# Layer 1 of a diffusion trunk: the prompt's attention, the new keys and the gate rows between the value projection's matmuls

## The reference, cut to what matters

```
q, k, v = split(h @ w_qkv + b_qkv, 3)                 # h: 384 modulated tokens
# prompt tokens (128): they see the prompt's keys only
p = softmax(q_p k_p^T / 8);  o_p = p v_p
new_k, new_v = k_p, v_p                               # outputs, too
# sample tokens (256): 256 local keys with a bias table, and 128 cached keys
p = softmax([q_s k_s^T / 8 + bias, q_s k_cache^T / 8]);  o_s = p [v_s, v_cache]
x = LayerNorm(alpha * x + gate * (o @ w_out + b_out)) # gate from c_ctx (prompt), c (sample)
```

## Time and profile before

| | |
|---|---|
| median of three runs | 1072.79 us |
| profiled execution, its span (it has no other time of its own) | 1072.2 us |
| PE busy | 1007.3 us, 94% of the span |
| DVE busy | 606.4 us, 57% |
| POOL busy | 349.6 us, 33% |
| ACT busy | 216.6 us, 20% |
| HBM traffic | 296 GB/s over the span |
| stretch of the change | from 632.81 (value projection begins) to 741 us (last unit of the attention) |

### The profile page before, as it was taken

The page is one execution under the profiler, slowest core; times in us unless marked ns, Lnnn a source line. Parts: engine busy times, 40 slices in busy tenths (PEclk is TensorE's granted clock), DMA queues, the critical chain, the costliest instruction groups (busy, mean ns, idle before and its releaser), DMA issues.

```text
span 1072.2 us, 25725 instructions
## 1 busy us (share of the span) xinstructions
PE 1007.3 (94%) x10500; PEld 605.7 (56%) x10500; DVE 606.4 (57%) x1388; ACT 216.6 (20%) x515; POOL 349.6 (33%) x440
## 2 busy tenths in 40 slices
PE   8999997999899999999989999999988999999983
PEld 2555554565556656666555554576455666666651
DVE  6458899675743333333479992475665333333336
ACT  3343234003310000000140000463231000000002
POOL 1400051620145555545310000255013555554442
PEclk9999998999899999999989999799999999999997
DMA  9955547930999999999997787333078899999991
GB/s 329 401 231 181 211 156 278 403 94 28 362 401 405 407 406 406 349 405 405 371 380 279 268 326 288 128 99 99 0 266 357 309 406 405 393 384 405 405 384 64
DMA packets 101690, 318.22 MB, mean 297 GB/s; under 512 B 8402, under 2 KB 12690, under 8 KB 101235
## 3 DMA queue, kind: packets, MB, share of 16 engines
q1 hardware_dynamic: 91716, 298.87, 72.5%
q0 software_dynamic: 5776, 17.30, 4.8%
q10 hardware_dynamic: 4128, 1.05, 0.4%
HBM read 311.44 MB, written 5.77 MB: 296 GB/s over the span
## 4 chain that ended last, share of the span: by engine, by line
PE 73%; DVE 13%; SPq 4%; DMA 4%; issue 3%; POOL 2%; ACT 1%; DVEq 0%; ACTq 0%; POOLq 0%
PE bank L808 70%; SPq L517 4%; DMA ring<-in_moe_w_down 2%; DVE ring L1630 1%; PE bank L1264 1%; POOL P L782 1%; DVE st L2043 1%; DVE hT L1818 1%; DVE P L2103 1%; DMA group_row<-token_rows,rows_now 1%; DVE acc_odd L1730 1%; DVE uT L1741 1%; DMA row_beta<-in_ln_b 1%; ACT x L1434 1%; PE bank L1020 0%
## 5 line engine op out<-in xcount | busy, mean ns | idle before, releaser
L808 PE MATMUL bank<-ring,xgT 128*32 128x256 f32 x4224 | 241.2, 380 | 2.1 <-issue 1.5
L808 PE MATMUL bank<-hT,ring 128*128 128x384 f32 x640 | 209.8, 491 | 2.9 <-DVE hT L1818 2.9
L808 PEld LDWEIGHTS bank<-ring,xgT 128*32 128x32 f32 x4224 | 145.7, 110 | 79.6 <-issue 4.3
L2008 DVE TENSOR_TENSOR he<-sa,bank 128x128 f32<-128x128 f32 x66 | 19.0, 288 | 286.0 <-ACT sa L1480 286.0
L808 PEld LDWEIGHTS bank<-hT,ring 128*128 128x128 f32 x640 | 122.5, 192 | 89.6 <-issue 6.9
L1630 DVE CUSTOM_DVE_ANT_0 ring<-ring,ring 128x1024 f32<-128x1024 f32 x112 | 143.1, 1278 | 3.4
L808 PE MATMUL bank<-ring,heT 128*32 128x256 f32 x2112 | 129.0, 385 | 4.0 <-DMA ring<-in_moe_w_down 4.0
L808 PE MATMUL bank<-yg,ohT 32*128 32x256 f32 x1632 | 107.3, 391 | 3.2 <-DVE yg L2037 2.9
L763 POOL TENSOR_TENSOR yg<-ysb,gate_s 128x256 f32<-128x256 f32 x128 | 90.9, 732 | 44.9 <-ACT ysb L1485 44.8
L808 PEld LDWEIGHTS bank<-ring,heT 128*32 128x32 f32 x2112 | 63.0, 110 | 59.9 <-issue 26.6
L808 PEld LDWEIGHTS bank<-yg,ohT 32*128 32x128 f32 x1632 | 74.5, 184 | 36.1 <-issue 26.4
(11 more groups left out here) (294 smaller groups left out, 1138.3 us busy)
## 6 DMA issues: line engine op xcount, KB each, us to landing
ring<-in_moe_w_up SPq DMA_DIRECT2D x64, 2048.0 KB, 21.8
ring<-in_moe_w_down SPq DMA_DIRECT2D x32, 2048.0 KB, 15.5
ring<-in_k_ada SPq DMA_DIRECT2D x15, 2048.0 KB, 13.9
ring<-in_w_ada SPq DMA_DIRECT2D x9, 2048.0 KB, 16.4
ring<-in_na_w_qkv SPq DMA_DIRECT2D x6, 2048.0 KB, 13.0
ring<-in_hy_w_in SPq DMA_DIRECT2D x5, 2048.0 KB, 8.0
ring<-in_hy_w_out SPq DMA_DIRECT2D x2, 2048.0 KB
ring<-in_na_w_out SPq DMA_DIRECT2D x2, 2048.0 KB
```

Of the source, the lines that this page charges most:

```text
L808: return nc.tensor.matmul(out, lhsT, rhs, start=first, stop=last)
L2008: v.tensor_tensor(he[:], sa[:], ps[0][:, 128:256], ALU.mult).then_inc(S["he_ready"], 1)
```

## The change

The value projection is computed in another order, (h, t) = (0,0), (1,0), (0,1), (0,2), (1,1), (1,2), so that both halves of the prompt's values come first, and its 48 products are numbered by steps s. Between them stand, by step: scores of prompt unit n at s = 6 + 4n, its transposes at s = 12 + 4n, its product with the values at s = 14 + 4n; the new keys at s = 16, `gm1a` at s = 24, and the scores of the first sample unit at s = 44. `gm1b` follows the last value product, then sample units 9 to 23.

The value, key and gate groups now share banks 2, 3 and 5 (`SIDE_BANKS`) and wait for the group three numbers back; prompt units use banks 0 and 1 for scores, without alternation, so that `scores(n)` waits for the exponentials of unit n-1; both heads' transposes go to bank 4, and ACT copies both. `bv` moves to the place of the sample's gate row, so that the copy of `gm1b` waits for the last value group. The gate copies go from DVE to ACT. ACT's stores of the new keys and values move between the exponentials. SP's list is unchanged; `last_group` names the new last user of each slot (v_02 and v_12).

```diff
-                  ... ("qk", 16), ("v", 6), ("kctx", 2), ("gm1a", 2), ("gm1b", 2), *ending(1)]:
+                  ... ("qk", 16),
+                  ("v_00", 1), ("v_10", 1), ("kctx", 2), ("v_01", 1), ("gm1a", 2), ("v_02", 1), ("v_11", 1), ("v_12", 1), ("gm1b", 2),
...
+SIDE_AT, SIDE_END, SIDE_BANKS = G_AT["v_00"], G_AT["out1_00"], (2, 3, 5)
...
+    if SIDE_AT <= g < SIDE_END:
+        return SIDE_BANKS[(g - SIDE_AT) % 3]
...
+        Pp = at("Pp", [128, 3, 2, 128], RM + 4096)
-        bv = at("bv", [128, D], RM + 8192)
+        bv = at("bv", [128, D], o + 4096)
...
-                        return G_AT["qk"] + 4 * s + 3 if s < 4 else G_AT["v"] + TT * (s - 4) + TT - 1
+                        return G_AT["qk"] + 4 * s + 3 if s < 4 else G_AT[f"v_{s - 4}2"]
...
             def scores(u):
                 t, j = divmod(u, PAIRS)
-                if u >= 2:
-                    pe.wait_ge(p_ready if u - 2 < PAIRS else max_ready, 2 * (u - 1))
-                S = [ps[2 * (u % 2) + i] for i in range(2)]
+                if u == 0:
+                    wait_all_evacuated(pe, SIDE_AT)
+                elif u <= PAIRS:
+                    pe.wait_ge(p_ready, 2 * u)
+                elif u >= PAIRS + 2:
+                    pe.wait_ge(max_ready, 2 * (u - 1))
+                if u == PAIRS:
+                    pe.wait_ge(att_in, 48)
+                if u == PAIRS + 1:
+                    wait_all_evacuated(pe, SIDE_END)
+                S = [ps[2 * (u % 2) + i] if t > 0 else ps[i] for i in range(2)]
...
-            for n in range(units + 3):
+            for s in range(len(V_ORDER) * KT):
+                h, t = V_ORDER[s // KT]
+                k = s % KT
+                n = (s - 6) // 4
+                if s == 2 * KT:
+                    new_keys()
+                if s == 3 * KT:
+                    pe.wait_ge(mod_ready, 5)
+                    gates("gm1a", 1, 16, (0,))
+                if s >= 6 and s % 4 == 2:
+                    if n < PAIRS:
+                        scores(n)
+                    if 0 <= n - 2 < PAIRS:
+                        weigh(n - 2)
+                if s >= 12 and s % 4 == 0 and n - 1 < PAIRS:
+                    flip(n - 1)
+                if s == 44:
+                    scores(PAIRS)
+                if k == 0:
+                    i = W_AT[f"qkv_{4 + h}"]
+                    out = bank(G_AT[f"v_{h}{t}"])
+                    wait_weights(pe, i)
+                last = mm(out[:, :], hT[:, k, t * 128:(t + 1) * 128], w_view(i, 8, 512)[:, k, :], k == 0, k == KT - 1)
+                if k == KT - 1:
+                    last.then_inc(group_ready, 1)
+            gates("gm1b", 1, 16, (1,))
+
+            for n in range(PAIRS + 1, units + 3):
...
+            exponentials(PAIRS)
+            wait_evacuated(act, G_AT["v_12"])
+            gates_copied("gm1b", 1)
...
-            for n in range(units + 4):
+            for n in range(11):
+                if n < PAIRS:
+                    maximum(n)
+                    reciprocals(n)
+                if n == 10:
+                    maximum(PAIRS)
+                if n % 2 == 0:
+                    values(n // 2)
+                if n == 5 or n == 9:
+                    heads_out(n // 4 - 1)
+            reciprocals(PAIRS)
+            for n in range(PAIRS + 1, units + 4):
```

More of the change, by code:

```diff
@@ L780, in _ @@
                 pool.wait_ge(rden_ready, u + 1)
-                p = P[:, u % 3, 0, 0:n]
+                p = Pp[:, u % 3, 0, :] if u < PAIRS else P[:, u % 3, 0, 0:n]
                 nc.gpsimd.tensor_scalar_mul(p, p, den[:, 2 * u:2 * u + 1]).then_inc(scaled[0], 1)
@@ L804, in bank @@
                     wait_evacuated(pe, g - 8)
+                if SIDE_AT + 3 <= g < SIDE_END:
+                    wait_evacuated(pe, g - 3)
+                elif SIDE_AT <= g < SIDE_END:
+                    for before in range(SIDE_AT - 8, SIDE_AT):
+                        if bank_of(before) == bank_of(g):
+                            wait_evacuated(pe, before)
                 return ps[bank_of(g)]
@@ L1214, in _, with new_keys @@
                     last.then_inc(group_ready, 1)
[L1215 to L1222, removed]
-                    last.then_inc(group_ready, 1)
[L1225 to L1234, removed]
+            def new_keys():
+                for h in range(2):
+                    out = bank(G_AT["kctx"] + h)
+                    for j in range(4):
+                        last = nc.tensor.transpose(out[:, j * 128:(j + 1) * 128], kT[:, 4 * h + j, 0:128], ident[:])
+                    last.then_inc(group_ready, 1)
             units = TT * PAIRS
@@ L1259, in flip @@
                     pe.wait_ge(pt_ready[0], u)
-                    pe.wait_ge(pt_ready[1], u)
+                if u > PAIRS:
+                    pe.wait_ge(pt_ready[1], u - PAIRS)
                 for i in range(2):
-                    for c in range(1 if u < PAIRS else 3):
+                    if u < PAIRS:
+                        last = nc.tensor.transpose(ps[4][:, i * 128:(i + 1) * 128], Pp[:, u % 3, i, :], ident[:])
+                    for c in range(0 if u < PAIRS else 3):
                         cs = slice(c * 128, (c + 1) * 128)
@@ L1570, in turned @@
                     act.wait_ge(pv_done, u - 1)
-                nc.scalar.activation(PT[:, u % 2, 0, 0:n], ps[4][:, 0:n], ACT.Copy).then_inc(pt_ready[0], 1)
-            for n in range(units + 2):
+                if u < PAIRS:
+                    nc.scalar.activation(PT[:, u % 2, :, 0:128], ps[4][:, 0:256].rearrange("p (i n) -> p i n", i=2), ACT.Copy
+                                         ).then_inc(pt_ready[0], 1)
+                else:
+                    nc.scalar.activation(PT[:, u % 2, 0, :], ps[4][:, 0:384], ACT.Copy).then_inc(pt_ready[0], 1)
+            for n in range(PAIRS + 1):
+                if n == 3:
+                    keys_out()
+                if n == 4:
+                    values_out()
+                if n == 5:
+                    gates_copied("gm1a", 0)
+                if n < PAIRS:
+                    exponentials(n)
+                if n >= 1:
+                    turned(n - 1)
+            exponentials(PAIRS)
+            wait_evacuated(act, G_AT["v_12"])
+            gates_copied("gm1b", 1)
+            for n in range(PAIRS + 1, units + 2):
                 if n < units:
                     exponentials(n)
-                if n >= 2:
+                if n - 2 >= PAIRS:
                     turned(n - 2)
@@ L2077, in _, with values @@
             dve.wait_ge(att_in, 48)
-            for n in range(6):
-                g = G_AT["v"] + n
-                h, t = divmod(n, TT)
+            def values(n):
+                h, t = V_ORDER[n]
+                g = G_AT[f"v_{h}{t}"]
                 hs = slice(h * 512, (h + 1) * 512)
```

66 lines of the change are left out of this document (37 added, 29 removed).

## The result

The changed kernel takes 1087.04 us, the median of four runs (1085.19 to 1088.27), against 1072.88 us for the kernel before (1072.64 to 1075.36): 14.2 us slower, a ratio of 1.0116 with a 95% interval of 1.0102 to 1.0131. The profiled execution has a span of 1085.8 us, 13.6 us over the span before. The forecast was 1082.0 us, with a range from 1078 to 1087, so the measured time stands at its upper end.

What follows compares the result with a forecast made beforehand. PE was taken to bound the kernel (73% of the chain). A gain of 7.4 us without waits, against 5.0 + 2.6 and 9.1 us for two waits and the clock, gave 9.3 us later: 1082.0 us, range 1078 to 1087.

Steps and rivals of the forecast that it cites:

- What moves at no wait: Value projection with the prompt's work moved in: without any wait unit 9's scores come at 688.1 us, gaining 7.4 us.
- First wait, DVE's dot rows: Before unit 1's scores PE stands 5.0 us (4.6 to 5.4), since unit 0's maximum stands behind DVE's dot rows.
- The clock behind it: After PE's pause before unit 1's scores, about 5.2 us at the low clock lose 2.6 us.
- Second wait, the bias tables: The first bias table, queued behind the load that waits for v_12, lands at v_12 + 8.6 = 701.7 us.
- What hangs on the table: Unit 8's maximum, v_12's reading, gate copies and hand-offs: 3.1 us from the table to unit 9's scores at 704.8.
- From there to the end: From unit 9's scores on, low clock against no prompt work left: taken as 0, from -1 to +2 us.
- The sum: Unit 9's scores at 704.8 against 695.54 us, 9.3 us later, so a span of 1081.5 us.
- The median 0.6 us above the span: The whole kernel's median lies 0.6 us above the profile's span, so 1082.1 us, stated as 1082.0.
- Slower by more than I say: Rival, 9%: the low clock lasts some 10 us more in the mixed stage too, 1087 to 1095 us.
- Only DVE's wait: Rival: tables land before they are needed, 0.2 us later, 1073.0 us; 5% together with the tables' wait alone.
- The clock does not come back: Rival, 6%: small products and transposes hold PE's clock down, sample units take 5.2 us in place of 2.55; 1119 us.

Runs made afterwards that it cites:

- run 1: The changed kernel with the first three bias tables issued ahead of the load into the second value slot: 1080.57 us, ratio 1.0060 to the kernel before.
- run 2: The changed kernel with the maxima of units 0 and 1 taken between the last of DVE's dot rows: 1082.68 us, ratio 1.0080 to the kernel before.
- run 6: The changed kernel with all sixteen tables ahead of the load and the maxima of units 0, 1 and 2 before the last three dot rows: 1069.53 us.
- run 4: The kernel before, with the first three bias tables issued ahead of the load into the second value slot: 1073.13 us, ratio 0.9993.
- the repeat: The changed kernel measured once more, unedited: 1086.41 us, ratio 1.0108 to the kernel before.
- run 3: The changed kernel with the first three tables ahead of the load and the maxima of units 0 and 1 between the dot rows: 1075.42 us, ratio 1.0007.

## Why the prediction was right

The direction, both waits and the clock behind them held, and runs 1, 2 and 6 show each of them. The size was 5 us short in the median, at the upper end of the range, and that it did not leave the range is in part luck: misses of both signs cancel in the stretch, and the two parts outside it, put at nothing, both came out on the slow side. In the order of its steps:

- *What moves at no wait, 7.4 us to gain.* Right over the stretch by luck, and too large by 2.4 us at the instant that the prediction compares. With no waits (run 6) the stretch is 101.68 us against 109.14, 7.5 us less. Unit 9's scores come 57.7 us after the first value product, against 62.7 before: 5.0 us earlier, not 7.4. A prompt unit costs 660.48 to 665.12 = 4.64 us with four products in it, less 4 x 0.862: 1.19 us and not 0.96, 1.8 us for eight. The sample's stage gives the rest back, where the low clock and the leftover prompt work are gone from its beginning: 44.0 us from unit 9's scores to the output projection, 46.4 before. So the prediction's sentence that a shift of unit 9's scores is a shift of the end did not hold.
- *First wait, DVE's dot rows: 5.0 us.* 4.34 us in one profile, 5.43 in the other, 7.19 in run 1. What I had not said is that its end is fixed by DVE and its beginning by PE, so that the size depends on how early PE arrives. Run 2 shows the cause: with the maxima ahead of the last dot rows it is gone.
- *The clock behind it: 2.6 us.* It rose again at 653.8 us, 5.6 us after PE resumed, and the same instructions took 2.6 us longer than in run 2.
- *Second wait, the bias tables: v_12 + 8.6 us.* v_12 ended at 696.5, DVE went on at 705.47, 8.9 us later. Run 1 shows the cause, and run 4 that the cover, not the place, made it harmless before.
- *What hangs on the table: 3.1 us.* 3.0 us, from 705.47 to unit 9's scores at 708.49.
- *From there to the end: 0.* The sample's stage is 1.4 us shorter (753.49 - 708.49 = 45.0 us against 46.4), a little outside my bound of 1, and what follows it is 2.1 us longer: 0.7 us in sum, with the two parts of opposite sign.
- *The sum: 9.3 us later.* The stretch is 9.9 us longer (11.0 in the repeat). From the first value product to unit 9's scores it is 74.1 us, where I had 72.0. The mixed stage without waits is 2.3 us longer than I had (v_12 at 55.0 us in run 6, 52.7 predicted), the first pause with its clock 0.6 shorter, and the time from v_12 to unit 9's scores 0.4 longer. The term that was sized wrong is the prompt unit, 1.8 of the 2.3 us.
- *The median 0.6 us above the span.* Wherever one execution has both figures, its time is about 1.9 us above its span, so the profile of the kernel before was, by this estimate, an execution 1.2 us slower than its median, and the profile of the change one 0.6 us slower. That is why the medians differ by 14.2 us and the profiles by 13.6.

**What is missing, and where.** The medians differ by some 5 us more than the forecast of 9.3: 2.1 up to unit 9's scores, less 1.4 in the sample's stage, 2.1 behind the stretch, 1.6 ahead of it, and 0.6 between medians and profiles. Of the 13.6 us between the two profiles, 1.6 lie ahead of the changed stretch and are spread between runs. Some 2.1 us lie behind it, in both profiles of the change, where I had put nothing. For 0.8 us the traces have the chain. The load of `row_beta` (layer norm's beta) lands 7.0 to 7.2 us after issue in all seven profiles of the new order, and 6.3 us in both of the old. DVE's first work for the output waits for it, here before and after:

```profile
749.69 1.22 DVE L1843 TENSOR_TENSOR tmp<-gate,rows 128x1024 f32<-128x1024 f32 x1 [7.80 <-DMA row_beta<-in_ln_b]
762.03 1.23 DVE L1915 TENSOR_TENSOR tmp<-gate,rows 128x1024 f32<-128x1024 f32 x1 [8.60 <-DMA row_beta<-in_ln_b]
```

PE's pause behind the output projection's first part grows by the same amount, from 0.97 us to 1.77. The rest appears at the start of the expert stage, where the gathers of token rows landed 6.8 us after issue (median) in place of 4.9. Run 6 has both too, so they are not one of the two waits. Why these loads land later stays open; no run was made for it. In all, the part behind the stretch is 330.2 and 330.3 us in the two profiles of the old order and 331.1 to 334.3 in the seven of the new.

The Trainium skill's rule in "DMA: Bandwidth & Descriptors", section "Queues, rings and completion order", is the one that the prediction weighed for the table's landing: one issuer's descriptors are taken in ring order, and the engines take turns between issuers. The traces agree with both halves as far as they can show it. In the change the 2 MB load landed 7.9 us after its issue at 696.57, and the three tables behind it 8.2 us after theirs (median), which is later. The store of the new keys was not beside them there; before it was, and they took 8.8 us. The difference is 0.6 us, where the prediction reckoned with 1.3; no run moved the store alone. In run 1 the fourth table, behind the same 2 MB, was used 8.4 us after its issue. Its first three stood behind another load of 2 MB and landed 8.1 us after issue, in time for unit 8.

Of the rivals, none came true in its cause. *Slower by more than I say* begins at 1087 us, where the measured time is, but its cause, some 10 us more of low clock in the mixed stage, did not show: the clock was low there for 5.6 us, and the 5 us missing have the parts given above. *Only DVE's wait* is nearly the state of run 1: 6.6 us over the kernel before and not 0.2, since the fourth table and a longer first pause remained. *The clock does not come back* was wrong in both stages: it rose 5.6 us after the first pause and 3.0 us after the second.

## What to carry to other kernels

Before work is moved forward, list what its old place was covering: here the prompt's stage hid 8.6 us of a load queued behind another load, and that load's place cost nothing until the cover went. Look at the waits of all engines at the new place, not only of the one that is to be filled: a list in strict order (DVE's dot rows, SP's loads) may have to be reordered along with it. And one removed wait shows the next: the gain appeared only with the edits of run 6, when the reading of v_10 and the fourth table had been dealt with too.

## What the runs showed that I had not expected

- In the prompt's stage before, the clock stood at 0.50 for 16.6 us from 683 us on, with PE busy all the time; the same products between products of 128x512 ran at 1.00 for 57 us (run 6). What kept it low is not shown: run 6 has no pause ahead of them, and in the change small products alone followed the second pause and the clock rose after 3.0 us.
- A pause of 2.50 us before the third value group was followed by a low clock (run 3); one of 1.23 us at the same place was not (run 2). The length of a pause does not settle it (see also run 6, 2.15 and 2.13 us). Before the same transposes a pause of 1.90 us was followed by a clock of 0.50 in run 3 (1.54 us for six of them) and one of 1.88 us was not in run 1 (0.87 us for the same six):

```profile
707.00 0.87 PE L1279 MATMUL bank<-first,P 128*128 128x128 f32 x6 [1.88 <-POOL P L793]
```

- A pause that another engine ends hides what happens before it: PE's arrival at the first value product spread over 3.8 us (630.63 to 634.42), and the first pause took up most of the difference, 7.19 to 4.34 us.
